# Diff attention with its two maps on opposite halves of TensorE's rows, and a shorter GpSimd part in the recurrence's operands

## The reference, cut to what matters

```python
# time mix: the operands of the scan (512 tokens, 16 heads of 64)
zs = z + (jnp.pad(z, ((0, 0), (1, 0), (0, 0)))[:, :S] - z) * mu     # token shift
r, k, v, wd, ad, gd = _split(zs, (1024, 1024, 1024, 64, 64, 160))
decay = exp(-exp(-softplus(-(w0 + tanh(wd) @ w2)) - 0.5))
iclr = sigmoid(a0 + ad @ a2)
kk = heads(k * k_k); kk = kk / max(sqrt(sum(kk * kk)), 1e-12)
k = k * (1.0 + (iclr - 1.0) * k_a)
y = rwkv7_scan(r, decay, k, v, -kk, kk * iclr)
bonus = sum(r * k * r_k, per head) * v

# differential attention: 8 heads, each with two maps (q and k of 64 rows each),
# 512 tokens + 256 context tokens as queries; tokens see all 768 keys, context sees 256
s = einsum('bhmtd,bhmsd->bhmts', pair(qb), keys) * 64 ** -0.5       # m = 0, 1
p = softmax(s)
a = p[:, :, 0] - lam * p[:, :, 1]
o = einsum('bhts,bhse->bhte', a, vals)
```

## Time and profile before

| | |
|---|---|
| median of 3 runs | 5021.68 us |
| profiled execution | 5027.22 us, span 5025.7 us |
| TensorE matmul busy | 4512.4 us (90%), mean granted clock 0.929 |
| VectorE busy | 1990.7 us (40%) |
| ScalarE busy | 1495.6 us (30%) |
| GpSimd busy | 570.1 us (11%) |
| scores of both attentions, line 2132 | 144.1 us busy |

### The profile page before, as it was taken

How to read it: one execution, slowest core, us unless ns; L and a number is a source line. 1 busy time by engine, 2 the same in 40 slices (tenths; PEclk the granted TensorE clock), 3 DMA queues, 4 the chain that set the end, 5 groups by cost and what they waited for, 6 DMA issues and landing times. The chain is left out here.

```text
span 5025.7 us, 76868 instructions
## 1 busy us (share of the span) xinstructions
PE 4512.4 (90%) x33574; PEld 3491.4 (69%) x33574; DVE 1990.7 (40%) x3010; ACT 1495.6 (30%) x2619; POOL 570.1 (11%) x471
## 2 busy tenths in 40 slices
PE   6799899799968998999799869888889998788999
PEld 5576896577756766987576646455678887456877
DVE  4535334455335435344455332336431132334232
ACT  2533233322233432332323232035221121223221
POOL 1215100011002125000010000101000000032000
PEclk9899999899978998999899879799899999789999
DMA  3032002144322121012244211000011111101222
GB/s 135 26 104 68 28 4 97 63 168 169 112 75 73 51 97 68 4 41 99 96 167 150 83 47 51 21 30 1 26 47 63 63 59 55 46 9 34 96 89 84
DMA packets 97534, 351.87 MB, mean 70 GB/s; under 512 B 9904, under 2 KB 13488, under 8 KB 95792
## 3 DMA queue, kind: packets, MB, share of 16 engines
q1 hardware_dynamic: 86432, 313.01, 18.1%
q10 hardware_dynamic: 10768, 33.95, 1.8%
HBM read 332.24 MB, written 14.68 MB: 69 GB/s over the span
## 5 line engine op out<-in xcount | busy, mean ns | idle before, releaser
L289 DVE TENSOR_TENSOR wlo<-ring,whi 128x1024 fp32r<-128x1024 f32 x494 | 620.9, 1257 | 2055.4 <-ACT whi L279 2055.1
L279 ACT CAST whi<-ring 128x1024 fp32r<-128x1024 f32 x494 | 517.6, 1048 | 2523.6 <-PE ps L331 2111.4
L328 PE MATMUL ps<-h_hi,whi 128*128 128x512 f32 x1552 | 647.3, 417 | 48.2 <-DVEq L227 27.4
L331 PE MATMUL ps<-h_hi,wlo 128*128 128x512 f32 x1552 | 624.3, 402 | 0.0
L329 PE MATMUL ps<-h_lo,whi 128*128 128x512 f32 x1552 | 622.9, 401 | 0.0
L328 PE MATMUL ps<-hm_hi,whi 128*128 128x512 f32 (+1 forms) x1408 | 508.9, 361 | 50.5 <-POOL spread L1941 40.7
L329 PE MATMUL ps<-hm_lo,whi 128*128 128x512 f32 (+1 forms) x1408 | 483.4, 359 | 0.0
L328 PEld LDWEIGHTS ps<-h_hi,whi 128*128 128x128 f32 x1552 | 298.1, 192 | 195.6 <-issue 65.3
L331 PE MATMUL ps<-hm_hi,wlo 128*128 128x512 f32 (+1 forms) x1408 | 423.7, 358 | 0.0
L328 PEld LDWEIGHTS ps<-hm_hi,whi 128*128 128x128 f32 x1408 | 268.1, 190 | 134.3 <-POOL spread L1941 41.1
L328 PE MATMUL ps<-ac_hi,whi 128*128 128x512 f32 x880 | 332.5, 378 | 23.6 <-DVE ac_lo L483 22.8
(11 more groups left out here) (361 smaller groups left out, 7419.8 us busy)
## 6 DMA issues: line engine op xcount, KB each, us to landing
ring<-in_w SPq DMA_DIRECT2D x590, 512.0 KB, 3.3
x_spill<-x ACTq DMA_DIRECT2D x2, 2048.0 KB, 8.8
h_spill<-h ACTq DMA_DIRECT2D x2, 2048.0 KB, 6.3
m_spill<-m ACTq DMA_DIRECT2D x2, 2048.0 KB, 8.4
h_again<-h_spill ACTq DMA_DIRECT2D x2, 2048.0 KB, 7.7
ma<-m_spill ACTq DMA_DIRECT2D x2, 2048.0 KB, 10.4
x<-x_spill ACTq DMA_DIRECT2D x2, 2048.0 KB, 9.9
x<-in_x SPq DMA_DIRECT2D x1, 2048.0 KB, 10.4
```

Of the source, the lines that this page charges most:

```text
L279: self.A.copy(self.hi[k % 2][:], raw).then_inc(self.s_cut_hi.h, 1)
L289: self.V.tensor_tensor(self.lo[k % 2][:], raw, self.hi[k % 2][:].bitcast(F32), ALU.subtract).then_inc(self.s_cut_lo.h, 1)
L328: T.matmul(ps[:, b, 0:cw], hi, xh(q, c0, cw), start=q == 0, stop=False, skip_group_check=True)
L331: m = T.matmul(ps[:, b, 0:cw], lo, xh(q, c0, cw), start=False, stop=q == kt - 1, skip_group_check=True)
```

## The change

Four edits in the operands: GpSimd's difference is one instruction over 512 tokens, since `zb` gets a zero column in front (the copy writes to columns 1 to 512); the copy of the chunk decays is made by ScalarE right after the two exponentials; R's column stands one place ahead of V's (R0, R1, V0, R2, V1, ..., R7, V6, V7, and the weights are stored in that order); and the table `first` is (14, 15, 17, 18, 20, 21, 23, 24).

Differential attention gets its own function. The matmuls of the scores alternate between the maps (map 0 and map 1 on the first 512 keys, then both on the last 256). There are three pairs of PSUM banks for scores instead of two, so the scores of step s wait only for the exp of map 0 of step s-1. The transposes use one bank in two rounds of three blocks, the copy after each round is ScalarE's alone, and the values use one bank. The combine is one step later, map 0 has 4 buffers and map 1 has 3. The grouped-query layer keeps `attention`.

```diff
@@ recurrence_operands
-        zb = [self.view(f"zb{i}", 6144 + 6 * S + i * 512, 512) for i in range(2)]
+        zb = [self.view(f"zb{i}", TMP + 8192 + 2 * 520 + 2 * S + i * 520, 520) for i in range(2)]
-        part = [(None, n) for n in range(3)] + [(1, j) for j in range(DT)] + [(2 * x, j) for j in range(DT) for x in (0, 1)]
+        part = [(None, n) for n in range(3)] + [(1, j) for j in range(DT)] + [(0, 0)]
+        for j in range(1, DT):
+            part += [(0, j), (2, j - 1)]
+        part.append((2, DT - 1))
-        first = (14, 15, 17, 19, 21, 22, 24, 25)
+        first = (14, 15, 17, 18, 20, 21, 23, 24)
@@ act_exps
             A.activation(eN[i][:], AT[:, j, :], ACT.Exp, scale=DECAY_C).then_inc(self.s_te.h, 1)
+            A.wait_ge(self.s_te.h, b_te + j + 1)
+            A.copy(PC[:, :, j], eP[i][:, :, CH])
@@ pool_tick
-                G.tensor_tensor(dd[n % 2][:, 1:S], zb[n % 2][:, 0:S - 1], zb[n % 2][:, 1:S], ALU.subtract)
-                G.tensor_scalar(dd[n % 2][:, 0:1], zb[n % 2][:, 0:1], -1.0, None, ALU.mult).then_inc(self.s_dd.h, 1)
+                G.tensor_tensor(dd[n % 2][:], zb[n % 2][:, 0:S], zb[n % 2][:, 1:S + 1],
+                                ALU.subtract).then_inc(self.s_dd.h, 1)
...
-                G.tensor_copy(PC[:, :, j], eP[i][:, :, CH])
@@ new function
+    def diff_attention(self):
...
+        E = [[self.view(f"map0_{i}", TB2 + i * T2, T2) for i in range(4)],
+             [self.view(f"map1_{i}", TB2 + (4 + i) * T2, T2) for i in range(3)]]
+        rounds = [[(0, 3), (3, 6)] if n == T2 else [(0, n // P)] for n in keys]
...
+        def pe_scores(s):
+            h, qt = steps[s]
+            if s >= 1:
+                T.wait_ge(self.s_aexp.h, b_exp + 2 * s - 1)
+            segs = key_segments(first_key[s], T2)
+            for n, (c0, cw, b) in enumerate(segs):
+                for q in range(2):
+                    rows = slice(64 * q, 64 * q + 64)
+                    m = T.matmul(ps[:, 2 * ((2 * s + q) % 3) + n, 0:cw], Q2[rows, h, qt * P:(qt + 1) * P],
+                                 K2[rows, h, c0:c0 + cw], start=True, stop=True, skip_group_check=True)
+                    if n == len(segs) - 1:
+                        m.then_inc(self.s_asc.h, 1)
+        def pe_turn(s, r):
...
+            if r == 0:
+                T.wait_ge(self.s_acomb.h, b_comb + s + 1)
+            if at > 0:
+                T.wait_ge(self.s_apa.h, b_pa + at)
...
+        def pe():
+            pe_scores(0)
+            for t in range(N + 4):
+                if 3 <= t < N + 3:
+                    pe_turn(t - 3, 0)
+                if t >= 4:
+                    pe_values(t - 4)
+                if 3 <= t < N + 3 and len(rounds[t - 3]) > 1:
+                    pe_turn(t - 3, 1)
+                if t + 1 < N:
+                    pe_scores(t + 1)
+        def act():
+            for t in range(N + 4):
+                if 3 <= t < N + 3:
+                    act_copy(t - 3, 0)
+                if t < N:
+                    act_exp(t, 0)
+                if 3 <= t < N + 3 and len(rounds[t - 3]) > 1:
+                    act_copy(t - 3, 1)
+                if t >= 4:
+                    A.wait_ge(self.s_aval.h, b_val + t - 3)
+                    h, qt = steps[t - 4]
+                    A.copy(O2[:, h, qt * P:(qt + 1) * P], ps[:, 7, 0:P]).then_inc(self.s_ao.h, 1)
+                if t < N:
+                    act_exp(t, 1)
+        def dve():
+            for t in range(N + 2):
...                 # maximum of map 0 of step t; reciprocals of step t-1; maximum of map 1 of step t
+                if t >= 2:
+                    s = t - 2
+                    V.wait_ge(self.s_awgt.h, b_wgt + s + 1)
+                    V.scalar_tensor_tensor(e(s, 0), e(s, 0), stat[s % 4][0][:, 2:3], e(s, 1), ALU.mult,
+                                           ALU.add).then_inc(self.s_acomb.h, 1)
@@ diff_layer
-        self.attention([(h, qt) for h in range(DT) for qt in range(6)], parts, 64 ** -0.5, combine, weigh,
...
+        self.diff_attention()
```

More of the change, by code:

```diff
@@ L24 @@
 NQH, NKVH, HD = 16, 4, 64
+DIFF_HD = 64
 CH = 64
@@ L900, in recurrence_operands @@
         AT, BB, BON = ops[:, 3 * DT:4 * DT, :], ops[:, 4 * DT:5 * DT, :], self.X
-        kn, kf, dd = ([self.view(f"{n}{i}", 6144 + (2 * x + i) * S, S) for i in range(2)]
-                      for x, n in enumerate(("kn", "k_f", "dd")))
-        zb = [self.view(f"zb{i}", 6144 + 6 * S + i * 512, 512) for i in range(2)]
+        kn, kf, dd, sq = ([self.view(f"{n}{i}", 6144 + (2 * x + i) * S, S) for i in range(2)]
+                          for x, n in enumerate(("kn", "k_f", "dd", "kk_sq")))
         eP = [self.view(f"e_p{i}", TMP + 8192 + i * 520, NCH, CH + 1) for i in range(2)]
         eN = [self.view(f"e_n{i}", TMP + 8192 + 2 * 520 + i * S, S) for i in range(2)]
-        sq = [self.view(f"kk_sq{i}", TMP + 8192 + 2 * 520 + (2 + i) * S, S) for i in range(2)]
+        zb = [self.view(f"zb{i}", TMP + 8192 + 2 * 520 + 2 * S + i * 520, 520) for i in range(2)]
         tb = sq
@@ L927, in recurrence_operands @@
         at_bonus = {n + 2: j for j, n in enumerate(first)}
-        def shifted(j_part):
-            p, j = j_part
-            return 3 + j if p == 1 else 3 + DT + 2 * j + p // 2
+        shifted = part.index
         def pe_low(j):
@@ L997, in act_tick @@
                     A.wait_ge(self.s_shift.h, b_sh + n - 1)
-                A.copy(zb[n % 2][:], ps[:, n % 3, :]).then_inc(self.s_zb.h, 1)
+                A.copy(zb[n % 2][:, 1:S + 1], ps[:, n % 3, :]).then_inc(self.s_zb.h, 1)
             if n == 1:
@@ L1081, in pool_tick @@
         def pool_tick(n, value):
+            if n == 0:
+                G.wait_ge(self.s_ones.h, ones_at + 1)
             if n < N:
@@ L1109, in recurrence_operands @@
         V.tensor_scalar(ka1, self.p1("k_a", 0, 8), -1.0, 1.0, ALU.mult, ALU.add)
+        V.memset(zb[0][:, 0:1], 0.0)
+        V.memset(zb[1][:, 0:1], 0.0)
         V.memset(eP[0][:, :, 0:1], 1.0)
@@ L2337, in diff_layer @@
         self.fence()
-        def parts(step):
-            h, qt = step
-            s0 = 0 if qt < 4 else S
-            r = [slice(0, 64), slice(64, 128)]
-            return [(Q2[r[u], h, qt * P:(qt + 1) * P], (lambda c0, cw, u=u: K2[r[u], h, c0:c0 + cw]), s0)
-                    for u in range(2)]
-        def weigh(E, st, n):
-            return G.tensor_scalar(E[1][:, 0:n], E[1][:, 0:n], st[1][:, 2:3], lam[:, 5:6], ALU.mult, ALU.mult)
-        def combine(E, st, n):
-            return V.scalar_tensor_tensor(E[0][:, 0:n], E[0][:, 0:n], st[0][:, 2:3], E[1][:, 0:n], ALU.mult, ALU.add)
-        self.attention([(h, qt) for h in range(DT) for qt in range(6)], parts, 64 ** -0.5, combine, weigh,
-                       lambda step, b: VTM[:, b, step[0] * P:(step[0] + 1) * P],
-                       lambda step: O2[:, step[0], step[1] * P:(step[1] + 1) * P])
+        self.diff_attention()
         self.norm_outputs()
@@ L2634, in layout @@
         ws.append(_tiles(low))
-        ws += [_tiles(rkv[:, D:2 * D]), _inter(rkv[:, :D], rkv[:, 2 * D:])]
+        rv = _inter(rkv[:, :D], rkv[:, 2 * D:]).reshape(2 * DT, DT, P, P)
+        order = [0] + [n for j in range(1, DT) for n in (2 * j, 2 * j - 1)] + [2 * DT - 1]
+        ws += [_tiles(rkv[:, D:2 * D]), rv[order].reshape(-1, P, P)]
         ws += [_tiles(gb), _tiles(f["w_o_rw"][l]), _tiles(f["w_out"][l])]
```

76 lines of the change are left out of this document (75 added, 1 removed).

## The result

| | before | after |
|---|---|---|
| median of 4 runs each, same chip | 5023.18 us | 4990.48 us (4988.69 to 4992.37) |
| ratio | | 0.9934, 95% interval 0.9917 to 0.9951 |
| profiled execution | 5027.22, span 5025.7 | 4992.37, span 4990.9 |
| first scores to what follows differential attention | 211.44 us | 184.71 us |
| operands, first copy to `zb` to first product of the scan, layers 1 and 2 | 201.52, 201.56 us | 198.12, 198.09 us |

The forecast was 4991 us. They repeat to about 0.1 us where neither the program in them nor the clock differs, while whole runs of one kernel scatter by 4 to 8 us.

The account below looks back on a forecast made before the run. It took a scores-maximum-exp chain alternating with TensorE's queue to bound attention, and a GpSimd-VectorE loop the operands from column 15. Savings of 23.5 (27.2 - 1.7 - 2) and 7 us, 30.5 off 5021.7, gave 4991 us, range 4978 to 5006.

Parts of the forecast that it names:

- The head: Differential attention: one head takes 22.0 us instead of 25.5, with four long ticks of 3.95 and short ones of 3.35 and 2.85.
- the slow start: First steps of differential attention at the low TensorE clock: may last one or two ticks longer, costing 2 us, bounds 0 and 8.
- The chain of 3.95: Attention's long ticks: scores, maximum of map 0, exp, next scores take 3.95 us, which stays and sets the tick.
- The drain: End of differential attention, last scores to what follows: added copy rounds and the deeper pipeline's step cost 1.7 us.
- In a long step the second map rides along: Attention's scores: alternating halves let both maps overlap, so a long step's scores take 1.45 us instead of 2.47.
- The one-column operation: Operands: GpSimd's one-column operation is in the pace-setting loop; removing it saves 12 ticks of 0.21, 2.5 us a layer.
- The copy: Operands: GpSimd's copy of the decays mostly waits for VectorE; removing it saves 0.4 us a layer, upper bound 6.2.
- The order: Operands: the new column order costs 4.4 us in the ticks and gains 4.9 at the end, together 0.5 a layer.
- Freed GpSimd: Operands rival: GpSimd gets its lock first, the copy's whole 6.2 us is saved, 9.2 a layer; total 4980, chance 0.15.
- Poorer attention: Attention rival: longer slow start, or GpSimd's weighing collides with the combine; gain 12 us instead of 23.5, total 5003, chance 0.14.
- No overlap: Attention rival: alternating products do not overlap, a head takes 26 us, attention 8 us longer; total 5023, chance 0.05.
- the slow clock: Attention rival: TensorE's clock falls to 1.2 GHz and stays, a head takes 32.7 us; total 5073, chance 0.04.

Follow-up runs that it names:

- Version 6: Kernel after with differential attention's combine, transposes and values each one tick earlier, as in the kernel before: 4990.46 us, ratio 0.9938, attention 181.23 us.
- Version 3: Kernel after with the scores' matmuls in the old order, map 0 whole and then map 1: 4994.15 us, ratio 0.9947, attention 184.71 us.
- version 5: Kernel before with the two maps' score matmuls alternating, still two pairs of banks: 5044.97 us, ratio 1.0045, attention 232.79 us.
- version 4: Kernel after with scores map by map and map 1's scores again waiting for the previous step's map 1 exp: 5043.32 us, ratio 1.004, attention 235.92 us.
- version 7: Kernel after with the copy of the decays back on GpSimd: one execution, operands 199.27 and 199.32 us.
- Version 2: Kernel before with only the four operand edits, old attention: 5014.57 us, ratio 0.9988, operands 198.08 and 198.11 us.
- version 1: Kernel before with only the new differential attention, old operands: 5001.75 us, ratio 0.996, attention 184.40 us.
- version 8: Kernel after with the difference's first column again a separate GpSimd operation: one execution, 4985.03 us, operands 200.02 and 200.14 us.

## Why the prediction was right or wrong

**The place and the sum.** 30.5 us were forecast, 23.5 and 7. The distances gave 26.7 and 6.9, of which 2.8 were lost again behind attention. The medians of the result differ by 32.7, the spans by 34.8; 3.6 of the spans' difference lie ahead of the first operands, where other versions with the same program start at 313.6 to 318.2 us, so that this is scatter. The hit to 0.5 us is in part luck: attention gave 3.2 more than forecast, what follows it took 2.8 back, and neither was foreseen; and the kernel before's median rose by 1.5 with its fourth run while the fall came out 2.2 larger than forecast.

**The head.** 22.0 was forecast, 21.5 measured (3.88, 3.16, 2.84 for 3.95, 3.35, 2.85). Up to the last scores before took 203.7, after 173.9: 29.8 less instead of the 25.2 that 27.2 and the slow start's 2 make. The chain of 3.95 was the right limit, and it kept its three parts within 0.07 us.

**The drain and the start.** 1.7 was forecast, 10.83 - 7.75 = 3.1 came. Version 6, one step shallower, needs 7.99 from its last scores (3493.65) to what follows (3501.64). So the added step costs 2.84 of the 3.1, just the short tick that it adds at the end, and the copy rounds 0.24; the step is the term that was priced too low. The other 0.6 of version 6's 3.5 lie ahead of its last scores. The slow start cost 1.3 more than before (173.88 - 8 x 21.52 + 2.84 = 4.6 against 3.3) for the forecast 2.

**The reason.** This is the step that failed: "In a long step the second map rides along" was put down to the alternating order. Version 3 shows that the order gives nothing, version 5 that without a third pair it costs 21 us, version 4 that the wait which the third pair removes is worth more than the whole gain in the queue order of the kernel after. The number was right since 1.45 (1.56 measured) did not depend on who lets map 1 start; that the change brought the third pair along with the new order is luck, as the prediction gives it no part. The rows that could have told it were in hand: map 1's first pass at 3367.55 was read as a hint of overlap and I did not ask what it had waited for, though ScalarE's timeline has the end of an exp right there. And "in a short step both maps' scores together take 0.70" is so only in the second short step (3380.41), in the old order; in the first, map 1 starts 0.92 after map 0, behind an exp. What the runs leave open is how much of the gain the transposes' two rounds and the copies on ScalarE give; no version tried the third pair with the old transposes, which use the bank it takes. That the third pair is the gain rests on the others being ruled out (the order by version 3, the deeper pipeline by version 6) and on the waits in the kernel before, not on a version with this pair alone.

**The operands.** The one-column operation: 2.5 forecast, 1.9 to 2.05 measured. The copy: 0.4 forecast, 1.2 measured, with the upper bound 6.2 excluded, as the reading of the product that lasts until L289 ends said. The order: 0.5 forecast, 0.1 measured. Together 3.4 forecast, 3.25 by the single steps and 3.4 and 3.5 by the whole. The last difference was to start near 514 and the scan near 517; they start at 510.05 and 513.52, of which 3.6 is the earlier start of the operands. (The Trainium skill, SBUF — State Buffer, SBUF: two separate sides, has the loser of the lock blocked for a whole instruction; version 7's groups agree for 4.7 of 6.4 us, and so do the ends of lines 1098, 290 and 1099 at 482.18, 483.26 and 484.39.)

**The rivals.** Freed GpSimd fell with version 7. Poorer attention: VectorE's combine beside GpSimd's weighing is stretched from 1.01 to 1.46 once a head, as its mechanism said, but in a short tick, outside the chain. No overlap and the slow clock did not come; a clock of 0.67 over 60 us appeared in version 4, whose scores hold TensorE with a wait inside them.

**What was not foreseen.** Behind attention the program takes 1487.3 us instead of 1484.5, and the difference is there by the next copy of the same name:

```profile
3503.57 1.03 POOL L1947 COPY spread<-con 16x1024 f32<-16x1024 f32 x1 [5.76 <-ACTq L229]
...
4250.30 1.03 POOL L1947 COPY spread<-con 16x1024 f32<-16x1024 f32 x1 [745.70 <-DMA tab<-in_tab]
```

746.73 us against 743.96 before (3541.24 to 4285.20). Its first 80 us, before and after (columns as in the earlier trace rows):

```profile
3541.24:3621.24 80.00, 68.56 (x267) 46.00 (x268) 29.55 (x37) 18.91 (x22) 1.02 (x1) 0.81 0.06 20
3503.57:3583.57 80.00, 68.55 (x255) 44.70 (x256) 28.93 (x36) 17.86 (x21) 1.03 (x1) 0.79 0.06 20
```

TensorE is busy just as long and gets through 255 of the same matmuls instead of 267, at a granted clock of 0.79 instead of 0.81. Over the whole stretch it is busy 686.9 instead of 683.9 us with the same 3792 matmuls, and that is the difference. So it is the clock that takes it; what makes the clock fall otherwise stays open. Version 2 has 744.10 for the stretch, version 1 745.47, but version 1 gets it back later: behind attention they take 1484.4 (version 1) and 1484.5. The nine other versions that have both halves of the change take 1486.9 to 1487.7, with attentions from 181 to 236 us, so it does not hang on how long attention takes.

## What to carry to other kernels

Ask of every matmul that starts late which semaphore it waits for, before giving the credit to the order: on opposite row halves TensorE ran the products side by side out of program order as soon as no wait stood between them, and here a third pair of buffers, which removes that wait, is what the runs leave as the gain. Where a chain over several engines sets the tick, shorten the chain or the drain; shorter work on one engine only helps down to the chain's length (version 5: scores of 1.56, ticks of 4.94). Work moved off GpSimd or VectorE while the two share a loop is to be priced by what the other one then takes, and differences of a few microseconds in 5000 are to be read between fixed instructions, not from totals.

## What the runs showed of the hardware

- Two maps' products of 64 rows each, in the order map 0, map 1, take 1.57 us for a long step where a wait between them makes it 2.55; their passes start in pairs (3377.01 twice).
- In the kernel after's first layer VectorE's L290 is 1.22 long alone and mostly 2.20 to 2.31 beside GpSimd, GpSimd's product of line 1099 is 1.45 to 2.28. Where they meet, one ends 1.1 after the other (483.26 and 484.39).
- The same instructions between two unchanged points took 1262.6 us in the kernel after (513.52 to 1776.16) and 1257.2 in version 8. TensorE is busy 1148.4 and 1142.0 us in them with the same 11498 matmuls, so the clock makes the difference; the mean granted clocks of the two whole executions are 0.929 and 0.931. What sets the clock differently is open.
